# Trainium2: one decoder layer, the first feed-forward product by seven half products in place of eight, its output through memory, and the delta rule's exchange stored tile by tile

## What is computed

```python
mixed = jnp.concatenate([oa, ob, oc], axis=-1).astype(x.dtype)
o = mixed @ P['w_out'][l]
x = x + (gate1 * rmsnorm(o, P['g_post_mix'][l])).astype(x.dtype)

h = (rmsnorm(x, P['g_pre_ffn'][l]) * (1.0 + scale2) + shift2).astype(x.dtype)
up = h @ P['w_up'][l]                                  # (1088, 1024) @ (1024, 2 * 2816)
up, ffn_conv_new = causal_dwconv(up, ffn_conv_prev, P['ffn_conv_w'][l])      # 3 taps
a, b = jnp.split(up.astype(f32), 2, axis=-1)
y = (jax.nn.gelu(a) * b).astype(x.dtype) @ P['w_down'][l]
x = x + (gate2 * rmsnorm(y, P['g_post_ffn'][l])).astype(x.dtype)
```

```python
diff = gc[..., :, None] - gc[..., None, :]
decay = jnp.where(tri, jnp.exp(jnp.where(tri, diff, 0.0)), 0.0)
lower = jnp.where(strict, jnp.einsum('bhncd,bhnsd->bhncs', kb, k) * decay, 0.0)
sol = lax.linalg.triangular_solve(lower + jnp.eye(C, dtype=lower.dtype), rhs, left_side=True, lower=True)
```

## Time and profile before

| | |
|---|---|
| time, median of 3 runs | 1884.64 us (1882.75 to 1889.18) |
| the profiled execution | 1892.74 us, span 1891.0 us |
| busy in the span: TensorE, VectorE, ScalarE, GpSimd | 89%, 45%, 30%, 27% |
| mean granted TensorE clock | 0.931 |
| delta rule | 666 to 912 us |
| first feed-forward product | 1054 to 1599 us |
| second feed-forward product | 1599 to 1891 us |

### The profile page before, as it was taken

The page is one execution under the profiler, slowest core; times in us unless marked ns, Lnnn a source line. Parts: engine busy times, 40 slices in busy tenths (PEclk is TensorE's granted clock), DMA queues, the critical chain, the costliest instruction groups (busy, mean ns, idle before and its releaser), DMA issues. The chain is left out here.

```text
span 1891.0 us, 27374 instructions
## 1 busy us (share of the span) xinstructions
PE 1689.3 (89%) x10269; PEld 1494.8 (79%) x10269; DVE 857.1 (45%) x1434; ACT 573.7 (30%) x931; POOL 509.1 (27%) x721
## 2 busy tenths in 40 slices
PE   4789978999688877999698599999999997999997
PEld 2568876899466666898576599999999996878776
DVE  1561017630555434555334255555555554454544
ACT  2432132221344332222233233333333332232322
POOL 1431022321100027763023233333333332111111
PEclk7899988999799888888799799999999998999999
DMA  8425422220311068232322211111111111444544
GB/s 314 136 97 190 151 97 72 80 82 14 134 59 38 19 180 206 70 99 63 141 88 74 71 45 44 44 43 39 41 43 44 44 44 58 147 156 143 172 141 142
DMA packets 121346, 182.89 MB, mean 97 GB/s; under 512 B 31620, under 2 KB 89780, under 8 KB 117938
## 3 DMA queue, kind: packets, MB, share of 16 engines
q1 hardware_dynamic: 118802, 172.89, 28.8%
q10 hardware_dynamic: 2464, 8.91, 1.2%
HBM read 151.00 MB, written 30.65 MB: 96 GB/s over the span
## 5 line engine op out<-in xcount | busy, mean ns | idle before, releaser
L2257 PE MATMUL fu_ps<-h_hi,fu_whi 128*128 128x364 f32 (+1 forms) x1056 | 234.5, 331 | 13.4 <-ACT fu_whi L2305 13.4
L2257 PE MATMUL fu_ps<-h_lo,fu_whi 128*128 128x364 f32 (+1 forms) x1056 | 234.2, 330 | 0.0
L2257 PEld LDWEIGHTS fu_ps<-h_hi,fu_whi 128*128 128x128 f32 x1056 | 184.4, 189 | 13.6 <-ACT fu_whi L2305 13.6
L2257 PEld LDWEIGHTS fu_ps<-h_lo,fu_whi 128*128 128x128 f32 x1056 | 184.3, 189 | 0.0
L2262 PE MATMUL fu_ps<-h_hi,fu_wlo 128*128 128x364 f32 (+1 forms) x1056 | 183.1, 329 | 0.0
L2262 PEld LDWEIGHTS fu_ps<-h_hi,fu_wlo 128*128 128x128 f32 x1056 | 176.9, 188 | 0.0
L2503 PE MATMUL fd_ps<-fd_whi,fd_yhi 128*128 128x512 f32 x396 | 124.8, 397 | 21.7 <-DVE fd_wlo L2565 16.2
L2311 ACT ACTIVATE fu_zp<-fu_ps 128x728 f32<-128x728 f32 x44 | 34.3, 780 | 357.3 <-PE fu_ps L2262 357.3
L2275 POOL TENSOR_TENSOR fu_wlo<-fu_w,fu_whi 128x1024 fp32r<-128x1024 f32 x44 | 117.6, 2675 | 87.0 <-ACT fu_whi L2305 87.0
L2528 ACT ACTIVATE fd_whi<-fd_w 128x1024 fp32r<-128x1024 f32 x66 | 69.9, 1061 | 196.6 <-PE fd_ps L2503 172.8
L2503 PE MATMUL fd_ps<-fd_wlo,fd_yhi 128*128 128x512 f32 x396 | 123.4, 393 | 0.0
(11 more groups left out here) (322 smaller groups left out, 3128.5 us busy)
## 6 DMA issues: line engine op xcount, KB each, us to landing
fd_w<-in_w_down SPq DMA_DIRECT2D x66, 512.0 KB, 3.5
wa<-in_w_ada SPq DMA_DIRECT2D x24, 1024.0 KB, 6.8
fu_w<-in_w_up SPq DMA_DIRECT2D x44, 512.0 KB, 3.4
fp_w<-in_w_fm SPq DMA_DIRECT2D x16, 512.0 KB, 3.5
scr_la<-dr_la SPq DMA_DIRECT2D x16, 384.0 KB, 4.0
dr_la<-scr_la SPq DMA_DIRECT2D x16, 384.0 KB, 5.5
scr_qkv<-fp_y SPq DMA_DIRECT2D x9, 544.0 KB, 2.6
dr_stg<-scr_qkv SPq DMA_DIRECT2D x8, 576.0 KB, 5.9
```

The lines of the kernel that those rows point to most:

```text
L2257: pe.matmul(ps[slot][:, n, 0:size], w_hi[:, slot, kk, :], h[:, kk, c:c + size], start=(kk == 0 and h is K.h_hi), stop=False)
```

## The change

Three edits are made at once.

**First product.** A pair of tiles is taken as a 2x2 block product: the two feature tiles, the inner dimension in halves of 512 and the tokens in halves of 544. Winograd's form of Strassen's scheme makes it from 7 half products in place of 8. The four combinations of the activations (`T1` to `T4`) are made once at the start and split (`factors`, `whole`, `low4`: VectorE, GpSimd, ScalarE); the four combinations of the weights are made for each pair on GpSimd (`front_sums`, `back_sums`); all seven weight operands are split, the high parts on ScalarE, the low parts on GpSimd. Pair 0 is made in the plain way (`plain`). Each half product is 4 blocks x 3 cross products x 2 column pieces (272 and 272, or 240 and 304), 24 matmuls, into one of four PSUM buffers; VectorE adds them up from PSUM. The raw weights of a pair are loaded with two DMAs into one buffer. The output tile goes to memory, `scr_y`. All loops are written out. `conv` keeps its six instructions.

**Second product.** It reads its input back from `scr_y` (ring of four buffers), delays the end of a pass by two slices into the next one, and takes a fourth PSUM buffer for the first tile of the last pass.

**Delta rule.** q, k, v are stored unit by unit, so that one partition's piece is contiguous; `dr_la` holds its two halves apart, and one of them is stored with a partition's data contiguous. The decay rows are mixed once by a product (`mix`), split into three bf16 parts that are stacked on 76 partitions, and the 12 decay matmuls of a unit take bf16 operands.

```diff
 def delta_rule(nc, ctx, K):
+        parts = sb("dr_parts", [SPLIT, TOK], BF16)
...
-                sp.dma_start(stg[:, i % 3, :, 0:n], K.scr_qkv[:, :, c0:c0 + n]).then_inc(g_in[i % 3], 16)
+                sp.dma_start(stg[:, i % 3, :, 0:n], K.scr_qkv[SEQ_OF[i], :, :, 0:n]).then_inc(g_in[i % 3], 16)
...
+            def mix(p):
+                c, w = PIECES[p]
+                pe.matmul(mixed_in[p][0:2 * H, 0:w], dc[:, D_MIX:D_MIX + 2 * H], K.rows[:, c:c + w], start=True, stop=True).then_inc(mix_mm, 1)
...
-                            last = pe.matmul(ps[0:n, c:c + n], dc[:, o:o + n], K.rows[:, c0:c0 + n], start=False,
+                            last = pe.matmul(ps[0:n, c:c + n], sel16[:, 2 * h + a, 0:n], parts[:, c0:c0 + n], start=False,
...
-def ffn_up(nc, ctx, K, yT):
+def ffn_up(nc, ctx, K):
+        raw = sb("fu_w", [P, 2, KD, P])
+        w_hi = sb("fu_whi", [P, PROD, HK, P], F32R)
+        w_lo = sb("fu_wlo", [P, PROD, HK, P], F32R)
+        sums = sb("fu_s", [P, 2, HK, P])
+        tmp = sb("fu_tmp", [P, 9, HALF])
+        ps = [own.enter_context(nc.psum_tensor(f"fu_ps{i}", [P, 2, 512], F32)) for i in range(4)]
...
         def _(sp):
+            def load(j):
+                after(sp, lo_set, splits(j))
+                for m in range(2):
+                    sp.dma_start(raw[:, m], K.w_up_d[2 * j + m]).then_inc(raw_in, 16)
+            def store(j):
+                sp.wait_ge(y_set, j + 1)
+                sp.dma_start(K.scr_y[j], ybuf(j)).then_inc(K.y_kept[j % 2], 16)
...
+            for j in range(KF):
+                if 0 < j < KF - 1:
+                    load(j + 1)
+                if j:
+                    store(j - 1)
...
         def _(pe):
+            def product(q, o, part):
+                pe.wait_ge(lo_set, splits(q + 1) + o + 1)
+                lane_free(q, o)
+                for kk in range(HK):
...
+                    for m, (w, low) in enumerate(((w_hi, 0), (w_hi, 1), (w_lo, 0))):
+                        for n, (c, size) in enumerate(SPLIT[o]):
+                            last = pe.matmul(lane_of(q, o)[:, n, 0:size], w[:, o, kk], part(low, kk, slice(c, c + size)),
+                                             start=(kk == 0 and m == 0), stop=(kk == HK - 1 and m == 2))
...
+            for q in range(KF - 1):
+                product(q, A11, h_part(0, 0))
+                product(q, S2, t_part(T2))
+                product(q, S1, t_part(T1))
+                product(q, S3, t_part(T3))
+                product(q, A12, h_part(1, 0))
+                product(q, S4, h_part(1, 1))
+                product(q, A22, t_part(T4))
...
         def _(pool):
+            def lo(j, o):
+                n = splits(j) + (ORDER0.index(o) if j == 0 else o)
+                pool.wait_ge(hi_set, n + 1)
+                pool.tensor_tensor(w_lo[:, o], block_of(j, o), w_hi[:, o], ALU.subtract).then_inc(lo_set, 1)
+            def front_sums(j):
+                pool.wait_ge(raw_in, 32 * (j + 1))
+                pool.wait_ge(lo_set, splits(j))
+                pool.tensor_tensor(sums[:, 0], a21, a22, ALU.add).then_inc(s_set, 1)
...
+            for j in range(1, KF):
+                more = j + 1 < KF
+                if more:
+                    front_sums(j + 1)
+                halo(j, 0)
+                if more:
+                    lo(j + 1, A11)
+                    lo(j + 1, S2)
+                    lo(j + 1, S1)
+                    back_sums(j + 1)
+                halo(j, 1)
+                if more:
+                    lo(j + 1, S3)
+                copies(j, 1)
+                if more:
+                    lo(j + 1, A12)
+                    lo(j + 1, S4)
+                copies(j, 0)
+                if more:
+                    lo(j + 1, A22)
...
         def _(act):
+            for q in range(KF - 1):
+                j = q + 1
+                more = j + 1 < KF
+                evict_p1(q)
+                if more:
+                    hi(j + 1, A11)
+                gelu(j - 1)
+                if more:
+                    for o in (S2, S1, S3):
+                        hi(j + 1, o)
...
         def _(dve):
+            def factors(c):
+                dve.tensor_tensor(f12, K.h_hi[:, c, HALF:TOK], K.h_lo[:, c, HALF:TOK], ALU.add).then_inc(td, 1)
...
+            def add_even(q, o, dst, t):
+                return dve.tensor_tensor(even(dst), lane_even(lane_of(q, o)), even(t), ALU.add)
...
+            for q in range(KF - 1):
+                if q:
+                    make_c21(q - 1)
+                conv(q, 1)
+                make_u2(q)
+                make_u4(q)
+                product(q)
+                make_c22(q)
+                make_u3(q)
+                make_c11(q)
+                make_c12(q)
+                conv(q + 1, 0)
...
-def ffn_down(nc, ctx, K, yT):
+def ffn_down(nc, ctx, K):
-        RING = 2
+        RING, LEAD = 4, 3
+        OUT_BANK = ((0, 1, 2), (0, 1, 2), (3, 0, 1))
...
+                    sp.dma_start(yr[:, k], K.scr_y[f, :, c:c + W]).then_inc(yr_in[k], 32)
+                sp.dma_start(wd[:, k], K.w_down_d[f]).then_inc(w_in[k], 16)
...
+            for g in range(LAST):
+                part(g)
+                p, f = divmod(g, KF)
+                if p and f == LEAD - 1:
+                    for n, rows in enumerate(width(p - 1)[1]):
+                        finish(p - 1, n, rows)
```

More of the change, by code:

```diff
@@ L68 @@
 D_MASK8 = D_MASK + 2 * P
-D_END = D_MASK8 + 2 * NSAMP
+D_MIX = D_MASK8 + 2 * NSAMP
+D_END = D_MIX + 2 * H_A
 def constants():
@@ L1633, in _ @@
             pe.wait_ge(dc_in, 16)
+            for p in range(3):
+                mix(p)
             pe.wait_ge(m16_set, 1)
@@ new lines, in ffn_up, with ybuf, splits, block_of @@
+        block = own.enter_context(nc.Block())
+        p1, u2, u4 = tmp[:, 0], tmp[:, 1], tmp[:, 2]
+        def ybuf(j):
+            return flat(tmp[:, 3 + 2 * (j % 2):5 + 2 * (j % 2)])
+        def splits(j):
+            return 0 if j == 0 else 4 + PROD * (j - 1)
+        def block_of(j, o):
+            if j == 0 and o == A21:
+                return a21
+            return {A11: a11, S2: sums[:, 1], S1: sums[:, 0], S3: sums[:, 1], A12: a12, S4: sums[:, 0], A22: a22}[o]
+        ORDER0 = (A11, A12, A21, A22)
@@ L2266, in _, with plain @@
-            pairs(pe, tile)
+            def plain(m):
+                lanes = ((2 * m, EVEN, 0), (2 * m + 1, BACK, HALF))
+                o = (A11, A12) if m == 0 else (A21, A22)
+                for low in (False, True):
+                    for kk in range(KD):
+                        if kk % HK == 0:
+                            pe.wait_ge(lo_set if low else hi_set, 2 * m + kk // HK + 1)
+                        for h in (K.h_hi,) if low else (K.h_hi, K.h_lo):
+                            for lane, split, c0 in lanes:
+                                for n, (c, size) in enumerate(split):
+                                    last = pe.matmul(ps[lane][:, n, 0:size], (w_lo if low else w_hi)[:, o[kk // HK], kk % HK],
+                                                     h[:, kk, c0 + c:c0 + c + size],
+                                                     start=(not low and kk == 0 and h is K.h_hi), stop=(low and kk == KD - 1))
+                last.then_inc(mm0, 1)
@@ new lines, in h_part, with part, t_part @@
+            def h_part(half_k, half_t):
+                def part(low, kk, c):
+                    return (K.h_lo if low else K.h_hi)[:, HK * half_k + kk, HALF * half_t + c.start:HALF * half_t + c.stop]
+                return part
+            def t_part(n):
+                def part(low, kk, c):
+                    return (t_lo if low else t_hi)[:, n, kk, c]
+                return part
+            plain(0)
+            plain(1)
+            for q in range(KF - 1):
[6 more added lines that the diff above has]
+                product(q, A22, t_part(T4))
@@ new lines, in _ @@
+            whole(0)
+            lo(0, A11)
+            lo(0, A12)
+            whole(1)
+            low4(0)
+            lo(0, A21)
+            lo(0, A22)
+            pool.wait_ge(small_in, 32)
+            halo(0, 0)
+            halo(0, 1)
+            whole(2)
+            low4(1)
+            front_sums(1)
+            whole(3)
+            low4(2)
+            copies(0, 0)
+            low4(3)
+            lo(1, A11)
+            lo(1, S2)
+            lo(1, S1)
+            back_sums(1)
@@ new lines, in product, with ready, add_back @@
+            def product(j):
+                dve.wait_ge(conv_b_set, j + 1)
+                dve.wait_ge(gelu_set, j + 1)
+                dve.tensor_tensor(ybuf(j), ybuf(j), flat(tmp[:, 7:9]), ALU.mult).then_inc(y_set, 1)
+            def ready(q, o):
+                dve.wait_ge(mm, PROD * q + o + 1)
+            def add_even(q, o, dst, t):
+                return dve.tensor_tensor(even(dst), lane_even(lane_of(q, o)), even(t), ALU.add)
+            def add_back(q, o, k, t):
+                for dst, a, b in zip(z_back(k), lane_back(lane_of(q, o)), back(t)):
```

(18 more changed lines are left out.)

532 lines of the change are left out of this document (337 added, 195 removed).

## The result

The changed kernel takes 1917.24 us (median, 1915.74 to 1918.39) against 1886.91 for the kernel before in the same runs: a ratio of 1.015, 95% interval 1.0132 to 1.0169, so 1.5% slower. Forecast were 1990 us and a loss of 105; measured is a loss of 30.

What follows compares the result with a forecast made beforehand. GpSimd's work, the load it waits for and VectorE's SBUF instructions bound the first product, 28.5 us a pair: +117, second product -3, delta rule -9, +105 on 1892.74; less 8.1 to the median, 1990 us, range 1910 to 2045.

Steps and rivals of the forecast that it cites:

- The mechanism of the first product: First product: GpSimd's work, its wait for the weight load and VectorE's SBUF instructions set the pace, 28.5 us a pair.
- signs named beforehand: First product: stage about 660 us, 28 to 29 a pair, 64-column VectorE instructions above 1 us, matmuls 130 ns apart.
- The round, step by step: First product: time from one pair's last GpSimd low-part subtraction to the next pair's, 28.5 us, twenty times.
- VectorE's port time: First product: time VectorE's instructions with both operands in SBUF exclude GpSimd, 8.0 of the 28.5 us a pair.
- a lock held for the whole instruction: GpSimd and VectorE: an instruction with SBUF operands on one keeps the other out for its whole duration.
- the table load of 1.28 us: First product, ScalarE: a table load of 1.28 us before each gelu, which put VectorE's product at 9.4 us.
- The start of the stage: First product: factors end at 1103, pair 1's first low part comes at 1106 and its last at 1122.5.
- The second product: Second feed-forward product: -3 us, from -3.5 for waits of 0.8 and 2.31 and +0.5 for new loads.
- The delta rule: Delta rule: -9 us (bounds -13 and +3), substitution starting 2.5 earlier and waits of 2.5, 2.6 and 1.3 gone.
- the port is packed: First product rival: VectorE's work fills the load's gap, 24.8 us a pair, 1915 us in all; chance 0.10.
- The rival that TensorE stays the bound: First product: 21.8 us a pair if VectorE's share is under 1.4 of 9.6; 1830 us in all, chance 0.10.
- no exclusion: First product: 22 us a pair with TensorE never idle would show GpSimd and VectorE do not exclude each other.

Runs made afterwards that it cites:

- run 1: The changed kernel with a second raw-weight buffer, loads issued a pair ahead and T4's low part left out: 1877.8 us, ratio 0.9956.
- run 3: The changed kernel without the four 1024-column VectorE instructions with two SBUF operands in a pair's convolutions: 1864.9 us, ratio 0.9895.
- run 6: The changed kernel without GpSimd's four sums of weight blocks from pair 2 on, raw blocks used instead: 1845.5 us, ratio 0.9779.
- run 7: The changed kernel with two of three matmuls in each half product: 1910.3 us, ratio 1.0134.
- run 9: The changed kernel with raw weights loaded in quarters, every engine's order kept as in the changed kernel: 1875.3 us, ratio 0.9946.
- run 5: The changed kernel with raw weights loaded in quarters, each after its last reader, and a new order on GpSimd: 1844.3 us, ratio 0.9778.
- run 4: The changed kernel with the first product as before, finished tiles also stored; delta rule and second product edits stay: 1884.6 us, ratio 0.999.

## Why the prediction was wrong

**The mechanism of the first product was right.** GpSimd's round sets the pace, lengthened by the load it must wait for and by VectorE's instructions with operands in SBUF. Runs 1, 3, 6, 7 and 9 each take away one part of it and show it: the load, VectorE's long instructions, GpSimd's sums and TensorE's work, which alone was free. Of the signs named beforehand, the stage is 579 us instead of 660 and the rounds 24.8 instead of 28 to 29. The 64-column instructions are crossed in both forms (TENSOR_SCALAR 1.28, SCALAR_TENSOR_TENSOR 0.53 on average between 1133 and 1594), where both were to be above 1. Matmuls of a product start 126 ns apart for the 130 taken. What the mechanism had wrong is how long one instruction keeps the other engine out.

**The term that was mis-sized** is in "The round, step by step": "5.2 + 14.0 + 1.2 + 0.1 for GpSimd and 8.0 of VectorE's port time in it". Measured are 5.0 for the load, 14.9 for GpSimd's own work and 4.9 for what VectorE adds. The work in GpSimd's stretch was that forecast: the product, a first convolution, and part of the second add up to 1.29 + 2 x 0.755 + 2 x 0.24 + 3 x 1.285 + 3 x 0.28 = 8.0 us by their own durations. But they delayed GpSimd by 4.9, the sum of what its instructions took over their uncrossed time: 1.07 behind the product, 1.0 behind each of three long instructions, 0.33 and 0.44 behind the two of 0.76, almost nothing (0.08) behind the short ones. Only a part of a duration keeps the other engine out, and the sum took the whole. The prediction said that the trace agreed with a lock held for the whole instruction. Its own row says otherwise: before the change a copy of 16 columns that takes 0.20 uncrossed took 1.21 from 1105.45, a delay of 1.0 us by a VectorE instruction of 1.29. 3.65 us a round over twenty rounds is 73 of the 82 us by which the stage was overestimated.

Another step was off too, at no cost: the table load of 1.28 us ahead of each gelu isn't there. ScalarE has a single one in 1110 to 1590, and VectorE's product starts 6.7 us after time 0 for 9.4.

**The start of the stage** has the same fault. The last factor was forecast for 1103 and the first low part for 1106; the latter starts at 1093.1, and 5 of these 13 us are only that the stage begins earlier. The two engines alternate there:

```profile
1060.45 1.83 POOL L2448 TENSOR_TENSOR fu_tmp<-h_hi,h_lo 128x544 f32<-128x544 f32 x1
1062.26 1.84 POOL L2450 TENSOR_TENSOR fu_tmp<-h_hi,h_lo 128x544 f32<-128x544 f32 x1
...
1064.06 1.84 POOL L2454 TENSOR_TENSOR fu_tlo<-fu_tmp,fu_thi 128x544 fp32r<-128x544 f32 x1
```

```profile
1061.11 1.76 DVE L2596 TENSOR_TENSOR fu_tmp<-fu_tmp 128x544 f32<-128x544 f32 x1
1062.80 1.88 DVE L2598 TENSOR_TENSOR fu_tmp<-fu_tmp 128x544 f32<-128x544 f32 x1
1064.60 1.88 DVE L2600 TENSOR_TENSOR fu_tmp<-fu_tmp 128x544 f32<-128x544 f32 x1
```

One of each takes 1.80 us together, where 0.72 for VectorE alone (four of them from 1087.09 to 1089.83) and 1.36 for GpSimd alone (at 1074.61) make 2.08. That stretch, and the tail of 22.2 for 23, give the other 9 us of the 82.

**The second product** came out as forecast: 288.7 us for 292.1, -3.4 for -3. One wait is left of two, 4.67 us before 1725.60. Two small errors stand in the sum: the waits of 0.8 and 2.31 add up to 3.1 and not 3.5, and the first matmul comes 7.5 us after the stage's start for 6.2, 1.4 later where 0.5 was allowed for the new loads. After that no matmul waits for its input.

**The delta rule** didn't give its 9 us. Its stage takes 247.5 us in the changed kernel's profile and 240.6 to 247.5, 243.9 on average, over the eleven profiles with this edit, for 246.2 in the one of before: 2 us on average. Its first phase, in the orders of time of TensorE and GpSimd:

```profile
679.71 0.63 PE L1632 MATMUL dr_ps<-dr_mk,dr_id 128*128 128x512 bf16 x1
...
684.51 0.39 PE L1632 MATMUL dr_ps<-dr_mk,dr_id 128*128 128x512 bf16 x1
...
692.43 1.54 PE L1613 MATMUL dr_ps<-cst,dr_stg 128*128 128x128 f32 x6 [2.28 <-DMA dr_stg<-scr_qkv]
```

```profile
692.31 0.21 POOL L1425 TENSOR_TENSOR dr_bx<-dr_bm,dr_bt 24x15 f32<-24x15 f32 x1 [28.69 <-DMA dr_bm<-scr_la]
704.92 0.21 POOL L1425 TENSOR_TENSOR dr_bx<-dr_bm,dr_bt 96x15 f32<-96x15 f32 x1 [1.87 <-DMA dr_bm<-scr_la]
...
729.79 1.79 POOL L1545 TENSOR_TENSOR dr_T<-dr_td,dr_cst 128x768 f32<-128x768 f32 x1 [1.74 <-DMA dr_td<-scr_T]
734.67 1.80 POOL L1550 TENSOR_TENSOR dr_ot<-dr_la,dr_cst 128x768 f32<-128x768 f32 x1 [1.34 <-DMA dr_la<-scr_lq]
```

A unit takes 4.8 us for 6.0 (4.2 was said), but after three of them TensorE waits 2.3 for the next unit's load, and mixing the rows comes first (unit 0's first mask product starts 10.2 us after the stage for 8.3: 1.9 later, where 1.5 was taken). GpSimd's substitution starts 31.4 us after the stage's first instruction (660.9) where it was 31.3 (666.1): not 2.5 earlier, but no earlier at all. Its later waits were to go and stayed: 1.9 for 2.5, 1.7 for 2.6, 1.3 for 1.3. Of the 9 us, 1.9 are won when the second phase begins, 79.6 us after the stage's start for 81.4. They are lost again around 852 to 858, where TensorE is busy throughout with the granted clock at 0.50 (1.2 GHz): the work from 851.12 to 858.59 takes 3.0 us more than the same work of before, from 857.61 to 862.05 at a clock of 1.00 (2.4 GHz). In the 8 us before 852 TensorE had been busy for 7.6. The tables of stretches, first of the changed kernel, then of the one before:

```profile
852.00:858.00 6.00, 6.00 (x35) 5.88 (x34) 2.56 (x7) 0.98 (x2) 3.21 (x4) 0.50 0.23 82
```

```profile
850.00:862.00 12.00, 11.59 (x119) 10.96 (x120) 6.92 (x16) 4.07 (x10) 5.31 (x6) 1.00 0.44 127
```

The stage's length goes with the clock. Its mean over the stage is 0.80 in the two longest, of 247.5 us (the changed kernel and run 1), and 0.83 in the five shortest, of 240.6 to 242.5 (runs 7, 9, 3, 4 and 6); before it was 0.83 too, with 246.2. So at an equal clock the edit is worth some 4 to 5 us (an estimate from these stages), and in the changed kernel the lower clock takes that back. Why the clock falls isn't shown.

**The rival "the port is packed"** gave 1915 and a round of 24.8, and both were measured, but for another reason. The port is empty for 3.4 of 24.85 us, and when the load's gap is closed (run 5) the round falls to 21.3. Two errors cancelled in its sum: durations counted in full, and a gap taken as filled. The rival that TensorE stays the bound needed VectorE's share in GpSimd's round to be small; it is what run 5 reaches. The prediction would have read rounds of 22 us with TensorE never idle as "no exclusion"; run 5 has them with the exclusion in place (crossed instructions of 2.27 us for 1.29), so that sign was too coarse.
